# Winograd-form decoder layer on one core: all weight sums made additions, the third one moved to a GpSimd DMA

## What is computed

```python
h = rmsnorm(x, g_mix_pre)
proj = h @ w_in                       # q, k, v, B, C, u, two gates
a = window attention(q, k, v)         # window 128, sinks
b = B * causal_dwconv(C * u)
merged = sigmoid(ga + b0) * (a @ w_attn_branch) + sigmoid(gb + b1) * (b @ w_conv_branch)
x = x + rmsnorm(merged @ w_o, g_mix_post)
up, gt = split(rmsnorm(x, g_ffn_pre) @ w_ffn_up)
f = (gelu(causal_dwconv(up) + bias) * gt) @ w_ffn_down
x = x + rmsnorm(f, g_ffn_post)
x = x + sigmoid(x @ w_ple_gate) * (p @ w_ple)
```

## Time and profile before

| | |
|---|---|
| median of three runs | 2685.79 us |
| the profiled execution, its own time | 2684.27 us |
| its span, first to last instruction | 2682.5 us |
| TensorE matmul busy | 2665.0 us (99%), 20913 matmuls |
| VectorE busy | 2174.0 us (81%) |
| ScalarE busy | 1338.8 us (50%) |
| GpSimd busy | 162.2 us (6%) |
| granted TensorE clock, mean | 0.999 |
| DMA moved | 460.55 MB, mean 172 GB/s |
| DMA queue q1 (SyncE's) | 367.55 MB, 38.8% of 16 engines |
| DMA queue q0 (GpSimd's) | 90.86 MB, 15.2% of 16 engines |
| HBM read | 403.24 MB |

### The profile page before, as it was taken

One profiled execution on the slowest core, in us unless ns is written; L12 is line 12 of the kernel. 1 busy time (PEld: TensorE's weight loads), 2 busy tenths in 40 slices (PEclk: granted clock), 3 DMA queues, 4 the chain that ended last, 5 costly groups with the idle time before them and its releaser, 6 DMA issues.

```text
span 2682.5 us, 54969 instructions
## 1 busy us (share of the span) xinstructions
PE 2665.0 (99%) x20913; PEld 2599.8 (97%) x20913; DVE 2174.0 (81%) x3813; ACT 1338.8 (50%) x2427; POOL 162.2 (6%) x250
## 2 busy tenths in 40 slices
PE   9999999999999999999999999999999999999999
PEld 8999999999999999989999999999999999999899
DVE  5998888888844687898888888888888767789887
ACT  5444545555532255645555555555555453445354
POOL 0110000000000000000000000000000000000000
PEclk9999999999999999999999999999999999999999
DMA  6344333333443455555566555665568575575674
GB/s 223 134 144 131 125 115 119 131 131 130 158 154 138 138 152 170 207 198 157 159 202 199 168 177 165 187 198 174 155 198 292 160 252 158 156 213 167 224 268 143
DMA packets 151348, 460.55 MB, mean 172 GB/s; under 512 B 16442, under 2 KB 46914, under 8 KB 147809
## 3 DMA queue, kind: packets, MB, share of 16 engines
q1 hardware_dynamic: 125040, 367.55, 38.8%
q0 software_dynamic: 26000, 90.86, 15.2%
q10 hardware_dynamic: 144, 0.15, 0.0%
HBM read 403.24 MB, written 54.11 MB: 170 GB/s over the span
## 4 chain that ended last, share of the span: by engine, by line
PE 98%; DVE 2%; issue 0%; ACT 0%; DVEq 0%; POOL 0%; ACTq 0%; POOLq 0%
PE pair L1056 77%; PE pair L1140 7%; PE pair L1021 7%; PE pair L987 3%; PE pair L822 1%; PE pair L1110 1%; PE pair L874 1%; PE pair L895 1%; DVE v_lo L1882 0%; DVE lo L1980 0%; PE pair L884 0%; PE pair L953 0%; PE pair L811 0%; DVE nv_s L1662 0%; PE pair L1088 0%
## 5 line engine op out<-in xcount | busy, mean ns | idle before, releaser
L1056 PE MATMUL pair<-o_hi,v_hi 128*128 128x260 f32 x5778 | 1638.0, 283 | 1.6 <-DVE f_low L2426 0.9
L1056 PE MATMUL pair<-o_hi,v_lo 128*128 128x260 f32 x5778 | 1631.4, 282 | 0.0
L1217 ACT ACTIVATE v_hi<-s_raw 128x512 fp32r<-128x512 f32 (+1 forms) x1328 | 827.9, 626 | 1008.4 <-PE pair L1056 810.2
L1056 PE MATMUL pair<-lo,v_hi 128*128 128x260 f32 x4140 | 1169.5, 282 | 0.0
L1882 DVE TENSOR_TENSOR v_lo<-s_raw,v_hi 128x512 fp32r<-128x512 f32 (+1 forms) x1264 | 858.1, 681 | 304.3 <-ACT v_hi L1217 267.6
L1056 PEld LDWEIGHTS pair<-o_hi,v_hi 128*128 128x128 f32 x5778 | 1086.3, 188 | 13.6 <-issue 12.0
L1056 PEld LDWEIGHTS pair<-o_hi,v_lo 128*128 128x128 f32 x5778 | 1088.2, 188 | 0.0
L1056 PEld LDWEIGHTS pair<-lo,v_hi 128*128 128x128 f32 x4140 | 778.1, 188 | 0.3
L1056 PE MATMUL pair<-lo_E,v_hi 128*128 128x260 f32 x834 | 236.0, 283 | 0.0
L1056 PE MATMUL pair<-lo_A,v_hi 128*128 128x260 f32 x804 | 226.7, 282 | 0.0
L1217 ACT ACTIVATE v_hi<-s_one 128x512 fp32r<-128x512 f32 (+1 forms) x212 | 132.1, 626 | 179.3 <-PE pair L1056 153.0
(11 more groups left out here) (229 smaller groups left out, 2321.9 us busy)
## 6 DMA issues: line engine op xcount, KB each, us to landing
s_raw<-in_sstream SPq DMA_DIRECT2D x468, 512.0 KB, 4.6
s_one<-in_sstream POOLq DMA_DIRECT2D x146, 512.0 KB, 5.3
raw<-f_scr SPq DMA_DIRECT2D x12, 1040.0 KB, 7.4
s_raw<-in_sstream SPq DMA_DIRECT2D x32, 384.0 KB, 4.1
g_scr<-d_h SPq DMA_DIRECT2D x16, 520.0 KB, 2.7
g_in<-g_scr SPq DMA_DIRECT2D x32, 260.0 KB, 2.8
x_scr<-y_sb SPq DMA_DIRECT2D x8, 1040.0 KB, 4.9
s_one<-in_sstream POOLq DMA_DIRECT2D x16, 384.0 KB, 4.6
```

Of the source, the lines that this page charges most:

```text
L1056: mm = pe.matmul(out, wt[:, slot, kk * P:kk * P + P], r[:, k, :], start=j in (0, 1, 3) and k == 0 and n == 0, stop=k == nk - 1 and n == 2, ...
L1217: nc.scalar.activation(v_hi[:, n % 4, 0:width], src, ACT.Copy, scale=0.5 if u == "br" else 1.0).then_inc(v_hi_rdy, 1)
```

## The change

The output tile of the second row of the 2 by 2 form (d21, d22) is computed with its sign turned, so that s2 = s1 + W0, s3 = W0 + W2 and s4 = W1 + s2 are additions like s1. The signs are put right elsewhere: the activation sums are made with their operands exchanged, some as a SCALAR_TENSOR_TENSOR with a factor of -1 (new helper `less`); ScalarE's copy for j = 1 gets scale=-1; VectorE subtracts where it added, and copies with a TENSOR_SCALAR times -1 instead of a COPY. TensorE's matmuls are the same in number, shape and order. From the second unit of w_o on s3 is no longer made by VectorE: `add_first_sum` issues a third DMA, ahead of its two, that adds W0 from DRAM into the loaded quarter W2, after a wait for that load.

```diff
             def s3(u, h):
...
+                if u > U_O:
+                    return
                 loaded(u, 0)
-                dve.tensor_tensor(quarter(u, 2, h), quarter(u, 0, h), quarter(u, 2, h), ALU.subtract)\
+                dve.tensor_tensor(quarter(u, 2, h), quarter(u, 0, h), quarter(u, 2, h), ALU.add)\
                    .then_inc(s3_done, 1)
...
-                dve.tensor_tensor(quarter(u, 0, h), w_src(u, 1, h), quarter(u, 0, h), ALU.subtract)\
+                dve.tensor_tensor(quarter(u, 0, h), w_src(u, 1, h), quarter(u, 0, h), ALU.add)\
                    .then_inc(s2_done, 1)
...
-                dve.tensor_tensor(quarter(u, 1, h), quarter(u, 1, h), quarter(u, 0, h), ALU.subtract)\
+                dve.tensor_tensor(quarter(u, 1, h), quarter(u, 1, h), quarter(u, 0, h), ALU.add)\
                    .then_inc(s4_done, 1)
...
+            def less(out, a, b):
+
+                return dve.scalar_tensor_tensor(out=out, in0=a, scalar=-1.0, in1=b,
+                                                op0=ALU.mult, op1=ALU.subtract)
...
-                dve.tensor_tensor(raw_of(s, 2)[:, k, :], raw_of(s, 5)[:, k, :], raw_of(s, 1)[:, k, :],
-                                  ALU.subtract).then_inc(t2_done, 1)
+                less(raw_of(s, 2)[:, k, :], raw_of(s, 1)[:, k, :], raw_of(s, 5)[:, k, :]).then_inc(t2_done, 1)
...
-                            dve.tensor_copy(d21, x_bank(u)).then_inc(c21_out, 1)
+                            dve.tensor_scalar(d21, x_bank(u), -1.0, None, ALU.mult).then_inc(c21_out, 1)
...
             def add_first_sum(u):
...
                 n = nk_of(u) * P
+                third = s_raw[r_of(u) % 2][2][:, 0:n]
+                pool.wait_ge(s_rdy[r_of(u) % 2][2], 16 * (r_of(u) // 2 + 1))
+                pool.dma_start(third, sstream[r_of(u), 0, :, 0:n], accum_op=ALU.add).then_inc(s3_dma, 16)
                 w = u - 2 if u - 1 in PLAIN else u - 1
```

More of the change, by code:

```diff
@@ L326, in sum_ready_1, with sum_ready_3 @@
                 eng.wait_ge(s1_done, 2 * (u - earlier(u)) + h + 1)
+        def sum_ready_3(eng, u, h):
+            if u > U_O:
+                eng.wait_ge(s3_dma, 16 * summed(u))
+            else:
+                eng.wait_ge(s3_done, 2 * (u - earlier(u)) + h + 1)
         def split_of(units):
@@ L493, in build @@
         s1_dma = sem("s1_dma")
+        s3_dma = sem("s3_dma")
         s2_done = sem("s2_done")
@@ L1211, in v_high @@
                     sum_ready_1(act, u, h)
+                elif j == 4 and q is None:
+                    sum_ready_3(act, u, h)
                 elif q is None:
-                    act.wait_ge({2: s2_done, 4: s3_done, 5: s4_done}[j], 2 * (u - earlier(u)) + h + 1)
+                    act.wait_ge({2: s2_done, 5: s4_done}[j], 2 * (u - earlier(u)) + h + 1)
                 else:
@@ L1249, in copied @@
                 a, b = ((0, u % 2), (1, 1), (0, u % 2))[j]
-                nc.scalar.activation(dst, pair[a][:, b, 0:HALF], ACT.Copy).then_inc(done, 1)
+                nc.scalar.activation(dst, pair[a][:, b, 0:HALF], ACT.Copy,
+                                     scale=-1.0 if j == 1 else 1.0).then_inc(done, 1)
             def first_unit(s, evac):
@@ L1959, in t3 @@
                 k = halves(s, h)
-                dve.tensor_tensor(raw_of(s, 4)[:, k, :], raw_of(s, 2)[:, k, :], raw_of(s, 0)[:, k, :],
-                                  ALU.subtract).then_inc(t3_done, 1)
+                less(raw_of(s, 4)[:, k, :], raw_of(s, 2)[:, k, :], raw_of(s, 0)[:, k, :]).then_inc(t3_done, 1)
             def t4(s, h):
@@ L1966, in t4 @@
                 k = halves(s, h)
-                dve.tensor_tensor(raw_of(s, 6)[:, k, :], raw_of(s, 3)[:, k, :], raw_of(s, 2)[:, k, :],
-                                  ALU.subtract).then_inc(t4_done, 1)
+                less(raw_of(s, 6)[:, k, :], raw_of(s, 2)[:, k, :], raw_of(s, 3)[:, k, :]).then_inc(t4_done, 1)
             def o_low(s, j):
@@ L2425, in f_out @@
                 dst = fo if upper else f_low[:, k, :, :]
-                dve.tensor_tensor(dst[:, 0, :], ge[:, 0:HALF], x_bank(u), ALU.mult)\
-                   .then_inc(c21_out, 1)
+                if u in PLAIN:
+                    ins = dve.tensor_tensor(dst[:, 0, :], ge[:, 0:HALF], x_bank(u), ALU.mult)
+                else:
+                    ins = dve.scalar_tensor_tensor(out=dst[:, 0, :], in0=x_bank(u), scalar=-1.0,
+                                                   in1=ge[:, 0:HALF], op0=ALU.mult, op1=ALU.mult)
+                ins.then_inc(c21_out, 1)
                 dve.wait_ge(c22_out, u + 1)
@@ L2443, in form @@
                     dve.wait_ge(forms_rdy, n + 1)
-                    dve.tensor_tensor(f_diff[:, 0, :], fo[:, 1, :], b12, ALU.subtract)\
-                       .then_inc(forms_rdy, 1)
+                    less(f_diff[:, 0, :], b12, fo[:, 1, :]).then_inc(forms_rdy, 1)
                 if j == 6:
                     dve.wait_ge(forms_rdy, n + 2)
-                    dve.tensor_tensor(f_diff[:, 1, :], fo[:, 0, :], f_diff[:, 0, :], ALU.subtract)\
-                       .then_inc(forms_rdy, 1)
+                    less(f_diff[:, 1, :], f_diff[:, 0, :], fo[:, 0, :]).then_inc(forms_rdy, 1)
                 if j == 4:
                     dve.wait_ge(low_stored, 16 * lowers(t))
-                    dve.tensor_tensor(b11, f_diff[:, 0, :], b11, ALU.subtract).then_inc(forms_rdy, 1)
+                    less(b11, f_diff[:, 0, :], b11).then_inc(forms_rdy, 1)
             def up_evac(u, i):
```

20 lines of the change are left out of this document (11 added, 9 removed).

## The result

The changed kernel takes 2699.72 us, the median of five runs (2697.23 to 2703.58), against 2685.79 for the kernel before (2684.4 to 2686.41, five runs): a ratio of 1.0056, 95% interval 1.0046 to 1.0067. It is slower by 13.9 us, clear of noise. The profiled execution has its own time of 2699.56 us and a span of 2697.8.

The account below looks back on a forecast made before the run. TensorE was taken as the bound. Stalls of 8.9, 0.7 and 4.7, clock 2.0, and relief of 1.2 twice gave +13.9 on 2684.27, so 2698.2; with 1.5 for the median, 2699.7 us, range 2686.5 to 2711.

Parts of the forecast that it names:

- What bounds: Whole kernel: TensorE sets the pace at 0.120 us a matmul, VectorE is no second bound, time changes only where TensorE stands still.
- The signs at 0: Activation sums, ScalarE's copy and VectorE's TENSOR_SCALAR: the turned signs cost nothing, taken as 0.
- VectorE's relief at -1.2 and -1.2: Up start and the gate set's plain unit: taking s3 off VectorE shortens TensorE's idle by 1.2 us at each.
- Steady units at 0: Steady units: one more adding DMA each raises the DMA share from 0.60 to at most 0.76 and costs 0.
- U_DOWN + 1 at 8.9 and 1.0: First down set, second unit: s1 lands 10.0 us later, TensorE stalls 8.9 us, plus 1.0 for reduced clock.
- my push of 0.9: At U_DOWN + 1: the previous unit's third DMA was taken to delay the load of W2 by 0.9 us.
- U_DOWN + 9 and + 17 at 0.7: Second units of the other down sets: slack 4.1 us against delay of 4.0 to 10, together taken at 0.7 us.
- U_GATE + 3 at 4.7 and 1.0: Gate set: addition lands about 2581.5, wanted for j = 1 at 2578.3; stall 4.7 us, plus 1.0 for reduced clock.
- the ends that I gave: At U_GATE + 3: the stall's range, 0.2 us with quiet DMA prices to 10.2 us with 10.0 for each DMA.
- the quiet rival: Down and gate sets: transfers run side by side at quiet prices, no stalls, -1.2 to -3.8 us, 2682 to 2684; chance 0.15.
- The sum: Whole kernel: 8.9 + 0.7 + 4.7 + 2.0 - 1.2 - 1.2 = +13.9 us on the profiled execution, median 2699.7.

Follow-up runs that it names:

- the relief alone: Against the kernel before: turned signs, third sum s3 left out from the second unit of w_o on, made by neither VectorE nor a DMA; 2681.75 us, ratio 0.9988.
- the second profile of the change: The unaltered change measured again on another chip against the kernel before; 2697.26 us against 2684.8, ratio 1.0050.
- the whole traffic with the third at the end: The change with the third DMA and its wait moved behind the addition into s_one; 2682.72 and 2681.8 us, ratios 0.9991 and 0.9988 to the kernel before.
- the wait with the copy first: The change with GpSimd's order made wait for W2, copy into s_one, third DMA, addition; 2691.48 us, ratio 1.0025 to the kernel before.
- the third first and plain: The change with the third DMA copying W0 over W2 instead of adding, third sum left out; 2694.68 us, ratio 1.0033 to the kernel before.
- the wait alone: Against the kernel before: turned signs, s3 on VectorE, no third DMA, GpSimd still waits for W2 before the copy; 2690.21 us, ratio 1.0020.
- the signs alone: Against the kernel before: only the turned signs, s3 on VectorE, no third DMA and no wait on GpSimd; 2684.58 us, ratio 1.0000.
- the complement: The change with the third DMA behind the addition in all units except U_DOWN + 1 and U_GATE + 3; 2699.86 us, ratio 1.0056 to the kernel before.

## Why the prediction was right, point by point

- **What bounds.** Right. TensorE's pace did not change with VectorE 79% instead of 85% busy in the steady stretch, and the relief alone gave 3.2 us for the 88 that left VectorE.
- **The signs at 0.** Right: ratio 1.0000. The TENSOR_SCALAR took 422 ns where the COPY had taken 420.
- **VectorE's relief at -1.2 and -1.2.** The mechanism was right; the first term was mis-sized. At the up start the offset moved by -2.3, both pairs nearly, where I took half of one: VectorE is behind from s4 through g_half to f_low, so every instruction ahead counts in full. s1's later landing, which I had set against it, made TensorE wait 1.0 us at 1158.54 and cost nothing behind, since the wait on s4 shrank by as much. The gate's plain unit gave 0.7, not 1.2: 0.52 us of its idle stay, and no run shows for what. VectorE's relief of 105 us was 88, so that VectorE is busy 2086.5 us and not near 2069; the durations of its rows overlap, and those of the last down set are shorter, 128x384.
- **Steady units at 0.** Right, with the share at 0.75 where I had at most 0.76. The quietest additions land in 5.3 to 5.9 us, the third in 6.1 to 7.9, and the plain copy of 512 KB into `s_one` took 3.6 to 4.3 in the up set before (35 issues). The Trainium skill's fit of a GpSimd DMA ("DMA: Bandwidth & Descriptors", section "Anatomy of one DMA"), 2.0 us plus bytes at 436 GB/s, gives 3.2 us for 512 KB as an estimate. The trace does not agree: that is a little short for the plain copy and far too short for an addition, and the stalls that it would have left out came.
- **U_DOWN + 1 at 8.9 and 1.0.** The path was right, the sum 9.9 against 8.2 (6.7 in the second profile of the change). From TensorE's entry on, the copy came 6.8 us later (8.1 forecast), copy to addition 1.7 longer (1.9), the addition took 8.2 (8.0): s1 landed 8.6 later instead of 10.0. The 1.3 too much is my push of 0.9, which did not come: the load landed 12.8 after issue, less than before. The product that waited was j = 1, not j = 2 as I had it: j = 1 was needed 24 matmuls after the entry, at 2059.7, 3.1 us after its first half was ready, and the matmul also waited for a sum of VectorE (y_sb, L2176) behind the split, so 6.2 us. j = 2 would then have cost nearly one more microsecond at full clock (v_lo at 2067.8, wanted at 2066.8); the half clock hid it. The clock was at half, 1.2 GHz, through most of the idle and the first 2.8 us of work, as the stretches of the changed kernel at both places show (columns as in the earlier trace rows):

```profile
2059.90:2066.70 6.80, 2.79 (x13) 2.79 (x14) 3.17 (x6) 5.14 (x7) 0.56 (x1) 0.50 0.96 292
2592.40:2595.80 3.40, 3.40 (x18) 3.40 (x18) 3.40 (x7) 2.98 (x6) 0.56 (x1) 0.50 0.79 160
```

  The offset grew by 1.8 us behind the idle; some 0.9 of it is that wait on j = 2, which by this working would have come at full clock too.
- **U_DOWN + 9 and + 17 at 0.7.** Too small: 3.7 (1.1 in the second profile). The last set's second unit and the one behind it were both late (TensorE waits at 2399.1, 2401.7 and 2407.7, the longest 0.9 us), since a delay is handed on: seen from TensorE, the copy of U_DOWN + 18 went out 1.6 us later than before, and it took 6.5 us instead of 4.3 beside its own unit's third, so that its s1 landed 4.4 later. I had taken units one by one.
- **U_GATE + 3 at 4.7 and 1.0.** 5.7 against 6.4. Landing 26.5 us behind the entry into the set of products, forecast 26.3; the idle was 4.6 as forecast (4.7), the clock's part 1.6 where I took 1.0. Of the ends that I gave, the upper one does not follow from its terms: 10.0 for each DMA in the terms of the lower one gives 10.9 and not 10.2; and at the lower end the addition lands at 2577.0, not before the 2576.8 of the quiet rival. The forecast uses neither.
- **The sum.** The forecast of +13.9 for the profiled execution met +15.3 there, and the medians differ by 13.9. So the agreement of the medians is closer than the terms deserve: -1.1 at the up start and -1.7 at U_DOWN + 1 stand against +3.0 in the other down sets, +0.7 at U_GATE + 3 and +0.5 in the gate's plain unit. That errors of this size left 0.0 us between the forecast of 2699.7 and the median is luck; measured again, the change was 12.5 us above the kernel before.
- **What I had not separated.** I put the loss down to the wait and the sharing. The runs show a third part, the place in the queue. Against the kernel before of the same chip, the relief alone gives -3.2 us, the whole traffic with the third at the end -2.3 and -3.0, the wait with the copy first +6.2, the third first and plain +9.4, the third first and adding +13.9 and +12.5. So the traffic alone costs within 1 us, the wait together with a third that stands ahead of the addition some 9 (the wait with no third DMA at all costs 5.2), and the place ahead of the copy another 6 to 8, of which 3.0 to 4.5 hang on the third's being an adding DMA.

What stays open: why one place earlier in GpSimd's queue makes the copy land 2 us sooner; why the loss at U_DOWN + 9 to + 18 is 3.7 us in one profile of the change and 1.1 in the other; and how much of the size at U_DOWN + 1 hangs on the seven pieces of activations, which no run moved.

## What to carry to other kernels

When work goes from an engine into a queue that another chain already uses, ask first what stands behind it in that queue and whether its own wait is longer than theirs: with the same DMA the kernel lost 12 to 14 us when it stood ahead of a chain that needed no load, and gained 2 to 3 us when it stood behind it. A mean DMA share says little about such a place; look at the starts of the stages, where in this kernel the share is 1 and the loads are late. And a repair at the unit that stalls can hand the stall to the next unit, as it did here, so repair the order for all units and not for one.

## What the runs showed of the hardware

An adding DMA of 512 KB takes more of the DMA engines than a plain one: with one of either more for each unit of 20.16 us, the share of the 16 engines rose from 0.61 to 0.75 and to 0.67. At the same place in GpSimd's program the adding one landed 6.1 to 7.9 us after its issue (median 6.8) and the plain one 3.7 to 6.6 (median 5.2), 35 of each from 1300 to 2000 us.

What the half clock costs hangs on who else is late. At the up start the kernel before has the idle of 2.55 us and half clock behind it. The kernel with the wait alone has the same work there, an idle of 2.56 and one of 1.88, and full clock throughout; from the first matmul behind the plain products (1153.85 and 1154.34) to the second unit (1184.46 and 1184.95) both take 30.61 us. VectorE was the later one either way, and caught up while TensorE was slow. In the kernel with the signs alone the half clock came behind the second idle instead, and that cost 0.3 us. At the two stalls it did cost, and more than the 1.0 that I took. Behind the first matmul that had waited, the offset went on to grow by 1.4 us at U_GATE + 3 in the kernel with the wait alone (idle 3.1) and by 1.6 and 1.5 in the two profiles of the change (4.6 and 5.2). At U_DOWN + 1 it grew by 1.8 in both profiles of the change (6.2 and 4.7) and by 2.4 in the complement (8.4), with whatever the wait on j = 2 adds. The granted clock behind these idles was 0.50 or 0.51.
